# A two-stack transformer kernel: another entry to the first mixing layer, and the last output units by halves

## The chip, the cores and the metric

The kernel runs on one core of a Trainium2 chip. The metric is the device time of one execution in microseconds (us), as the median of several runs. The engines are called PE (TensorE's matmuls; PEld is its weight load), DVE (VectorE), ACT (ScalarE), POOL (GpSimd) and SP (SyncE, which only issues DMAs here). Each engine works through its own queue in order, and they meet at semaphores.

## The reference, cut to what matters

Two small transformers run one behind the other on 256 tokens of width 1024 (two token tiles of 128). The first has a pooling layer and an attention layer, each followed by a gated feed-forward (FFN) layer. The second has two "mixing" layers, again each with an FFN. The place that the change is about is where the two meet:

```python
# end of the first stack
x = x + swiglu(rmsnorm(x, norm_ffn[1]), ...)
x = rmsnorm(x, final_norm)
# start of the second stack
h = rms_norm(x, attn_norm[0])
proj = h @ w_in[0]
...
x = x + mix @ w_o[0]
```

Two norms stand here one behind the other. The kernel takes them together: with g the gain of `final_norm`, it needs mean(x²) and mean((x·g)²). The layer's input is x·g times a factor per token (from both sums) times the second gain; the residual stream is x·g times another factor per token (from mean(x²) alone).

## The kernel before

**Weights come in units.** All weights pass through three slots of 128x2048 floats (`raw`, loaded by SP's queue). ACT's `split` copies a unit rounded to `whi`, DVE subtracts (`wlo = raw - whi`, line 991), and PE multiplies the rounded and the rest part: three products in place of one. Slot of unit n is n % 3, so ACT may write `whi` of unit n only when PE has finished with unit n-3: `split` waits for the counter `units_used` (line 678 is its ACTIVATE). A load of unit n waits for DVE's subtraction of unit n-3. The latents' two units of a mixing layer are 1664 wide, all others 2048.

**End of a layer.** The last two units of every output product (of an FFN, lines about 1850, or of an attention, `last_two_by_tile`) are multiplied tile by tile. I call the first of the two units A and the last one B. For each tile and unit there are two halves of 512 columns with six matmuls each, so one tile is 24 matmuls. In tile 1 the order is A half 0, A half 1, B half 0, B half 1. `used` is counted for A when its half 1 is done. In five of the seven places the next layer's tile-0 transposes (line 1729) stand ahead of the last six matmuls. The two others are the end of FFN 1, ahead of the first mixing layer, where they come behind all of them, and the end of the kernel. DVE adds each finished half to `x` (`add_residual`, line 1001).

**Start of a layer.** ACT squares the halves of tile 0 (line 689, with a sum by row), then does the `split` of the new layer's second unit (which goes to the slot of A), then two copies of the transposed input, `h_out` (line 696, `h_both`), then tile 1's squares. DVE computes the mean square, POOL the power -0.5 (`rstd`), and DVE multiplies (`normalise`, line 1019) to `xn`, which PE transposes. PE's first pass over tile 0 needs both the rounded second unit (`hi_ready`) and tile 0's `h_out`.

**The first mixing layer's entry** (`final_norm_1` on DVE, the part `if l == 0` on ACT) is written by hand. DVE makes x·g into `xn` (line 1394), ACT squares halves of x and of x·g (line 866), DVE combines sums (lines 1400, 1403, 1404), POOL makes both factors at once (line 659), DVE multiplies `xn` in place (`mixer_input`, line 1412), and at the end four `residual_out` (line 1417) write the residual stream. PE's `latents` (line 1631) works through tile 0's three passes, with tile 1's transposes between them, then tile 1's.

SP's queue issues, behind unit 5 of this layer, two loads of score biases into `bias`, then unit 6.

Of the kernel before, what the change touches and what calls it, by code (L numbers as in the profile page):

```python
# [26 lines left out]
ALU = mybir.AluOpType  # L27
# [3 lines left out]
P = 128  # L31
T = 256
D = 1024
# [153 lines left out]
def bass_two_stacks(nc, a, c, out):  # L187
    ctx = ExitStack()
    with ctx:
# [27 lines left out]
        usq = sb("usq", [P, TT, 2])  # L217
# [52 lines left out]
        dsquare = xn[:, 0, HALF:D]  # L270
        bias_moba = bias[:, 0:16 * T].rearrange("p (h k) -> p h k", h=16)
# [169 lines left out]
        def _(sp):  # L441
# [110 lines left out]
            for l in range(2):  # L552
                for n in range(15):
# [116 lines left out]
        def _(act):  # L670
# [186 lines left out]
            def mix(l):  # L857
# [3 lines left out]
                if l == 0:  # L861
                    done = [16]

                    def next_square(src, t, h, acc):
                        act.wait_ge(squares, done[0])
                        act.activation(junk[:, :], src[:, t, h * HALF:(h + 1) * HALF], ACT.Square, scale=1.0 / 32,
                                       accum_out=acc[:, t, h:h + 1]).then_inc(squares, 1)
                        done[0] += 1

                    def square_x(t, h):  # L870
# [3 lines left out]
                        next_square(x, t, h, ssq)  # L874

                    def square_scaled(t, h):
                        act.wait_ge(scaled_ready, 2 * t + h + 1)
                        next_square(xn, t, h, usq)

                    for h in range(2):  # L880
                        square_x(0, h)
                        square_scaled(0, h)
                    split(u0 + 1)
                    h_out(6, 0, 0)
                    h_out(6, 0, 1)
                    square_x(1, 0)
                    square_x(1, 1)
                    square_scaled(1, 0)
                    square_scaled(1, 1)
                    for h in range(2):  # L890
                        h_out(6, 1, h)
# [3 lines left out]
                for ev in mix_script():  # L895
# [81 lines left out]
        def _(dve):  # L977
# [15 lines left out]
            def add_residual(version, t, h):  # L993

                if (t, h) == (1, 1):
                    dve.wait_ge(units_used, LAST_U[version] + 1)
                else:
                    dve.wait_ge(acc_ready, 3 * ACC_NO[version] + 2 * t + h + 1)
                xs = x[:, t, h * HALF:(h + 1) * HALF]
# [384 lines left out]
            def final_norm_1():  # L1384
# [3 lines left out]
                def scaled(t, h):  # L1388
                    cols = slice(h * HALF, (h + 1) * HALF)
                    if (t, h) == (0, 0):  # L1390
                        dve.wait_ge(gains_in[1], 16 * 3)
                        dve.wait_ge(xT_ready, 4 * (HT_NO[6] - 1))
                    dve.wait_ge(x_ready, 12 + 2 * t + h + 1)
                    dve.tensor_tensor(xn[:, t, cols], x[:, t, cols], gx[:, cols], ALU.mult).then_inc(scaled_ready, 1)

                def mean_squares(t):

                    dve.wait_ge(squares, 22 if t else 19)
# [4 lines left out]
                    then_wait(dve.tensor_scalar(msq[:, 6 + t:7 + t], msq[:, t:t + 1], EPS, usq[:, t, 0:1], ALU.mult, ALU.add))  # L1403
                    dve.tensor_tensor(msq[:, 6 + t:7 + t], msq[:, 6 + t:7 + t], usq[:, t, 1:2], ALU.add).then_inc(msq_ready, 1)

                def mixer_input(t, h):

                    cols = slice(h * HALF, (h + 1) * HALF)
                    if (t, h) == (0, 0):
                        dve.wait_ge(gains_in[0], 16 * 4)  # L1410
                    dve.wait_ge(rstd_ready, tile_no(5, t) + 1)
                    dve.scalar_tensor_tensor(out=xn[:, t, cols], in0=xn[:, t, cols], scalar=rstd[:, 6 + t:7 + t],
                                             in1=gz[:, cols], op0=ALU.mult, op1=ALU.mult).then_inc(xn_ready, 1)

                def residual_out(t, h):
                    cols = slice(h * HALF, (h + 1) * HALF)
                    dve.scalar_tensor_tensor(out=x[:, t, cols], in0=x[:, t, cols], scalar=rstd[:, t:t + 1],
                                             in1=gx[:, cols], op0=ALU.mult, op1=ALU.mult).then_inc(x_ready, 1)
# [744 lines left out]
```

## Time and profile before

| | us |
|---|---|
| median of 3 runs | 1132.6 |
| lowest, highest | 1132.23, 1134.55 |
| the profiled execution | 1133.23 |
| its span in the trace | 1131.4 |
| PE busy in it | 1116.1 (99%) |
| DVE busy | 783.3 (69%) |
| ACT busy | 533.9 (47%) |
| POOL busy | 109.0 (10%) |

The profiled execution took 1.8 us more than its span; that part lies outside the instructions. The mean granted TensorE clock was 0.997 of full speed. PE's stalls are few, so each engine's rows are read around those stalls and around places where another engine waits for PE.

### The profile page before, as it was taken

The page shows a single profiled execution, that of the slowest core. Times are in us where ns is not written, and L with a number is a line of the kernel's source. Part 1 is how long each engine was busy: PE and PEld are TensorE (multiplying, and loading weights), DVE is VectorE, ACT ScalarE, POOL GpSimd, SP SyncE. Part 2 cuts the span into 40 slices and gives each one's busy share as a digit, 9 for nine tenths or more (in the row PEclk, how much of TensorE's full clock was granted, in tenths as well). Part 3 has the DMA queues.
Part 4 walks back from the last instruction along what each step waited for, and adds up shares of the span by engine and source line. Part 5 has one row for each costly group of instructions (what it writes and reads, how often), then busy time and mean ns, then how long its engine had stood idle before and what let it go on. Part 6 is the DMA issues. An engine that isn't in the chain of part 4 may idle for free.

```text
span 1131.4 us, 16797 instructions
## 1 busy us (share of the span) xinstructions
PE 1116.1 (99%) x6452; PEld 970.6 (86%) x6452; DVE 783.3 (69%) x1022; ACT 533.9 (47%) x706; POOL 109.0 (10%) x200
## 2 busy tenths in 40 slices
PE   8999999999999999998999999999999999999997
PEld 7888888898888888887998888888899988888886
DVE  6766666767667666678677576666776866766665
ACT  5533333455654333345576543333456755333332
POOL 1000000000000000001770000000038400000000
PEclk9999999999999999999999999999999999999999
DMA  8765565663356555566963466565689444665551
GB/s 255 254 205 194 179 211 192 219 222 121 130 170 227 190 181 190 187 183 212 274 163 112 149 223 201 175 199 185 181 238 224 117 150 135 214 208 186 185 185 38
DMA packets 174152, 211.23 MB, mean 187 GB/s; under 512 B 22387, under 2 KB 157107, under 8 KB 174098
## 3 DMA queue, kind: packets, MB, share of 16 engines
q1 hardware_dynamic: 164322, 202.89, 56.9%
q0 software_dynamic: 9776, 7.62, 3.6%
q8 instruction: 35, 0.57, 0.2%
q14 instruction: 19, 0.16, 0.0%
HBM read 201.98 MB, written 1.16 MB: 180 GB/s over the span
## 4 chain that ended last, share of the span: by engine, by line
PE 94%; DVE 3%; ACT 1%; DMA 1%; issue 1%; POOL 0%; SPq 0%; DVEq 0%; POOLq 0%; ACTq 0%
PE bank L1592 25%; PE bank L1596 13%; PE bank L1566 13%; PE bank L1567 13%; PE bank L1568 13%; PE bank L1663 3%; PE bank L1872 2%; PE bank L1893 2%; PE bank L1605 1%; PE bank L1729 1%; PE bank L1903 1%; DMA raw<-in_pool_w 1%; DVE wlo L991 1%; PE bank L2112 1%; PE bank L1608 1%
## 5 line engine op out<-in xcount | busy, mean ns | idle before, releaser
L678 ACT ACTIVATE whi<-raw 128x2048 fp32r<-128x2048 f32 x178 | 338.8, 1907 | 383.1 <-PE bank L1596 245.5
L991 DVE TENSOR_TENSOR wlo<-raw,whi 128x2048 fp32r<-128x2048 f32 x172 | 393.0, 2287 | 151.0 <-ACT whi L678 151.0
L1592 PE MATMUL bank<-h_both,whi 128*128 128x512 f32 x1280 | 304.6, 390 | 0.0
L1592 PEld LDWEIGHTS bank<-h_both,whi 128*128 128x128 f32 x1280 | 237.7, 188 | 47.7
L1566 PE MATMUL bank<-whi,o_hi 128*128 128x512 f32 x448 | 176.2, 393 | 0.0
L1567 PE MATMUL bank<-wlo,o_hi 128*128 128x512 f32 x448 | 174.9, 390 | 0.0
L1568 PE MATMUL bank<-whi,o_lo 128*128 128x512 f32 x448 | 174.4, 389 | 0.0
L1596 PEld LDWEIGHTS bank<-h_both,wlo 128*128 128x128 f32 x1280 | 164.1, 191 | 6.2
L1596 PE MATMUL bank<-h_both,wlo 128*128 128x256 f32 x1280 | 166.0, 283 | 0.0
L1568 PEld LDWEIGHTS bank<-whi,o_lo 128*128 128x128 f32 x448 | 84.1, 188 | 18.0
L1566 PEld LDWEIGHTS bank<-whi,o_hi 128*128 128x128 f32 x448 | 84.3, 188 | 17.6 <-issue 1.3
L1567 PEld LDWEIGHTS bank<-wlo,o_hi 128*128 128x128 f32 x448 | 84.3, 188 | 15.5
L1190 DVE TENSOR_REDUCE pr<-bank 128x512 f32<-128x1024 f32 x40 | 49.0, 1224 | 47.6 <-PE bank L1596 47.6
L603 POOL TENSOR_TENSOR rstd<-msq,neghalf 128x1 f32<-128x1 f32 x16 | 9.2, 576 | 749.8 <-DVE msq L1007 749.8
L1195 DVE TENSOR_REDUCE pr<-bank 128x512 f32<-128x1024 f32 x36 | 44.1, 1225 | 43.1 <-PE bank L1596 43.1
L1566 PE MATMUL bank<-h_both,whi 128*128 128x256 f32 x192 | 55.3, 288 | 0.8 <-DVE wlo L991 0.8
L786 ACT ACTIVATE pr<-pr,negmax 128x256 f32<-128x256 f32 (+1 forms) x96 | 45.9, 480 | 19.3 <-DVE negmax L1277 19.3
L1567 PE MATMUL bank<-h_both,whi 128*128 128x256 f32 x192 | 54.3, 283 | 0.0
L1568 PE MATMUL bank<-h_both,wlo 128*128 128x256 f32 x192 | 54.3, 283 | 0.0
L1277 DVE CUSTOM_DVE_ANT_0 pr<-bank,bias 128x256 f32<-128x256 f32 (+1 forms) x96 | 32.8, 399 | 17.1 <-PE bank L1872 11.0
L1663 PE MATMUL bank<-whi,h_both 128*128 128x512 f32 x160 | 39.7, 395 | 0.4 <-ACT h_both L696 0.3
L1566 PE MATMUL bank<-whi,h_both 128*128 128x256 f32 (+1 forms) x128 | 38.9, 304 | 0.7 <-DVE h_both L1339 0.7
(201 smaller groups left out, 1335.3 us busy)
## 6 DMA issues: line engine op xcount, KB each, us to landing
raw<-in_w_gate_up SPq DMA_DIRECT2D x44, 1024.0 KB, 5.1
raw<-in_w_down SPq DMA_DIRECT2D x44, 1024.0 KB, 4.9
raw<-in_w_gate SPq DMA_DIRECT2D x22, 1024.0 KB, 5.4
raw<-in_w_up SPq DMA_DIRECT2D x22, 1024.0 KB, 5.4
raw<-in_w_in SPq DMA_DIRECT2D x18, 1024.0 KB, 7.4
raw<-in_w_o SPq DMA_DIRECT2D x12, 1024.0 KB, 5.5
raw<-in_w_kv SPq DMA_DIRECT2D x8, 1024.0 KB, 5.4
raw<-in_w_q SPq DMA_DIRECT2D x4, 1024.0 KB, 5.2
```

Of the source, the lines that this page charges most:

```text
L678: act.activation(whi[:, s, 0:w], raw[:, s, 0:w], ACT.Copy).then_inc(hi_ready, 1)
L786: e = act.activation(pr[:, s, q, 0:w], src, ACT.Exp, bias=negmax[:, s, q:q + 1], scale=-1.0 if biased else 1.0, accum_out=psumrow[:, s, q: ...
L991: dve.tensor_tensor(wlo[:, s, 0:w], raw[:, s, 0:w], whi[:, s, 0:w].bitcast(F32), ALU.subtract).then_inc(lo_ready, 1)
L1190: dve.tensor_reduce(gate32, halves(0), AX_X, ALU.add).then_inc(gate_sum, 1)
L1195: dve.tensor_reduce(up32, halves(2), AX_X, ALU.add).then_inc(up_sum, 1)
L1277: e = dve.tensor_tensor_reduce(pr[:, s, q, 0:w], bank[i % 2][:, q * T:q * T + w], biases[q], -1.0, BIG, ALU.add, ALU.min, negmax[:, s, q:q ...
L1566: pe.matmul(dst, ahi, bhi, start=first, stop=False)
L1567: pe.matmul(dst, ahi, blo, start=False, stop=False)
L1568: return pe.matmul(dst, alo, bhi, start=False, stop=last)
L1592: pe.matmul(bank[bk + jj][:, :], hi[:, kc, jj * P:(jj + 1) * P], h_both[:, kc, :, :].rearrange("p a t -> p (a t)"), start=(kc == 0), stop= ...
L1596: mm = pe.matmul(bank[bk + jj][:, T:2 * T], lo[:, kc, jj * P:(jj + 1) * P], h_hi[:, kc, :], start=False, stop=(kc == KC - 1))
L1663: mm = pe.matmul(bank[bk][:, :], h[:, kc, tile(t)], pair_of(w, n, kc), start=(first and kc == 0), stop=(last and kc == KC - 1))
```

## The change

It has two parts (the diff's pieces stand in the order buffer, SP, ACT, DVE, PE's latents, PE's last units of an attention; the end of an FFN gets the same order as these). **One**, at the first mixing layer's entry: x·g gets a buffer of its own, `x_gained`, in the first 2048 columns of `bias`; ACT squares a whole 1024-wide tile of it in one instruction (its output goes to `xn` as scratch), so one DVE combination falls away per tile; the four residual writes move from DVE to ACT, behind the latents' squares; DVE's and ACT's orders are rewritten; ACT's `split` of the second unit comes behind tile 1's sums; the latents' passes and transposes get another order; and SP's bias loads and the next `add_residual` wait for the residual writes. **Two**, at all ends of layers: tile 1's last two units go half by half, so the order is A half 0, B half 0, A half 1, (transposes), B half 1.

```diff
+        x_gained = bias[:, 0:TT * D].rearrange("p (t d) -> p t d", t=TT)
...
+                        sp.wait_ge(x_ready, 4 * 5)
                         for i, dst in ((0, bias_diff), (1, bias_dil)):
...
+                    def square_gained(t):
+                        if t == 0:
+                            act.wait_ge(xT_ready, 4 * (HT_NO[6] - 1))
+                        act.wait_ge(scaled_ready, 2 * t + 2)
+                        act.activation(xn[:, t, :], x_gained[:, t, :], ACT.Square, scale=1.0 / 32,
+                                       accum_out=usq[:, t:t + 1]).then_inc(squares, 2)
...
-                    for h in range(2):
-                        square_x(0, h)
-                        square_scaled(0, h)
-                    split(u0 + 1)
+                    square_x(0, 0)
+                    square_x(0, 1)
+                    square_gained(0)
+                    square_x(1, 0)
                     h_out(6, 0, 0)
                     h_out(6, 0, 1)
-                    square_x(1, 0)
                     square_x(1, 1)
-                    square_scaled(1, 0)
-                    square_scaled(1, 1)
-                    for h in range(2):
-                        h_out(6, 1, h)
+                    square_gained(1)
+                    split(u0 + 1)
+                    h_out(6, 1, 0)
+                    h_out(6, 1, 1)
...
+                        if l == 0:
+                            for t in range(TT):
+                                act.wait_ge(rstd_ready, tile_no(5, t) + 1)
+                                for h in range(2):
+                                    cols = slice(h * HALF, (h + 1) * HALF)
+                                    act.activation(x[:, t, cols], x_gained[:, t, cols], ACT.Copy, scale=rstd[:, t:t + 1]).then_inc(x_ready, 1)
...
                 split_half(MIX_U[0], 0)
                 mean_squares(0)
-                split_half(MIX_U[0], 1)
+                add_residual(4, 1, 0)
                 mixer_input(0, 0)
                 mixer_input(0, 1)
-                add_residual(4, 1, 0)
+                scaled(1, 0)
                 add_residual(4, 1, 1)
-                for h in range(2):
-                    h_lo_out(6, 0, h)
-                    scaled(1, h)
-                split_half(MIX_U[0] + 1, 0)
+                scaled(1, 1)
+                h_lo_out(6, 0, 0)
+                h_lo_out(6, 0, 1)
                 mean_squares(1)
-                split_half(MIX_U[0] + 1, 1)
-                for h in range(2):
-                    mixer_input(1, h)
-                for h in range(2):
-                    h_lo_out(6, 1, h)
-                for t in range(TT):
-                    for h in range(2):
-                        residual_out(t, h)
+                split_half(MIX_U[0], 1)
+                mixer_input(1, 0)
+                mixer_input(1, 1)
+                split(MIX_U[0] + 1)
+                h_lo_out(6, 1, 0)
+                h_lo_out(6, 1, 1)
...
+                if j == 6:
+                    wait_h(j, 0)
+                    latent_pass(u0, 0, h_lo, whi, range(KC))
+                    pe.wait_ge(lo_ready, u0 + 1)
+                    latent_pass(u0, 0, h_hi, wlo, range(0, LAT_K))
+                    transposes(j, 1)
...
-                for t in range(TT):
-                    for i in range(2):
-...
+                for i in range(2):
+                    pe.wait_ge(lo_ready, n + i + 1)
+                    pe.wait_ge(out_lo, ready[i])
+                    residual(n + i, chunks[i], O, False, i == 1, (0,))
+                for h in range(2):
+                    mm = residual(n, chunks[0], O, False, False, (1,), (h,))
+                    if h:
+                        used(mm)
+                        transposes(j, 0)
+                    mm = residual(n + 1, chunks[1], O, False, True, (1,), (h,))
+                used(mm)
```

ACT's queue at the first mixing layer's entry, before: the 1664-wide copy is the `split` of the layer's second unit.

```order
175 L866 ACTIVATE junk,ssq<-x 128x512 [waits squares,x_ready]
176 L866 ACTIVATE junk,usq<-xn 128x512 [waits squares,scaled_ready]
177 L678 ACTIVATE whi<-raw 128x1664 [waits units_used,raw_in0]
178 L696 ACTIVATE h_both<-bank 128x4x128 [waits xT_ready] x2
179 L866 ACTIVATE junk,ssq<-x 128x512 [waits squares,x_ready] x2
180 L866 ACTIVATE junk,usq<-xn 128x512 [waits squares,scaled_ready] x2
181 L696 ACTIVATE h_both<-bank 128x4x128 [waits xT_ready] x2
```

The same place after the change:

```order
175 L879 ACTIVATE xn,usq<-bias 128x1024 [waits scaled_ready,xT_ready]
176 L871 ACTIVATE junk,ssq<-x 128x512 [waits squares,x_ready]
177 L698 ACTIVATE h_both<-bank 128x4x128 [waits xT_ready] x2
178 L871 ACTIVATE junk,ssq<-x 128x512 [waits squares,x_ready]
179 L879 ACTIVATE xn,usq<-bias 128x1024 [waits scaled_ready]
180 L680 ACTIVATE whi<-raw 128x1664 [waits units_used,raw_in0]
181 L698 ACTIVATE h_both<-bank 128x4x128 [waits xT_ready] x2
```

The copy of the second unit stood ahead of tile 0's `h_out` and now stands behind them and behind tile 1's sums.

PE's queue from the first latents' pass on, before (`h_both` with `whi` or `wlo` are the latents' passes, `ident,xn` the transposes of tile 1):

```order
923 L1631 MATMUL bank<-whi,h_both 128x416 [waits hT_hi,hi_ready]
924 L1631 MATMUL bank<-whi,h_both 128x416 x3
925 L1631 MATMUL bank<-whi,h_both 128x416 [waits hT_hi]
926 L1631 MATMUL bank<-whi,h_both 128x416 x3
927 L1631 MATMUL bank<-wlo,h_both 128x416 [waits lo_ready]
928 L1631 MATMUL bank<-wlo,h_both 128x416 x3
929 L1631 MATMUL bank<-whi,h_both 128x416 [waits hT_lo]
930 L1631 MATMUL bank<-whi,h_both 128x416 x3
931 L1729 MATMUL bank<-ident,xn 128x128 [waits xn_ready]
```

And after:

```order
923 L1632 MATMUL bank<-whi,h_both 128x416 [waits hT_hi,hi_ready]
924 L1632 MATMUL bank<-whi,h_both 128x416 x3
925 L1632 MATMUL bank<-whi,h_both 128x416 [waits hT_hi]
926 L1632 MATMUL bank<-whi,h_both 128x416 x3
927 L1632 MATMUL bank<-whi,h_both 128x416 [waits hT_lo]
928 L1632 MATMUL bank<-whi,h_both 128x416 x7
929 L1632 MATMUL bank<-wlo,h_both 128x416 [waits lo_ready]
930 L1632 MATMUL bank<-wlo,h_both 128x416 x3
931 L1738 MATMUL bank<-ident,xn 128x128 [waits xn_ready]
```

Four more matmuls now stand ahead of tile 1's transposes; the first row waits for the same two semaphores as before, of which `hi_ready` is given by the copy that moved on ACT.

PE's queue at the end of FFN 0, tile 1, before (rows 230 to 235 are A half 0, row 242 begins B half 0):

```order
240 L1567 MATMUL bank<-wlo,o_hi 128x512
241 L1568 MATMUL bank<-whi,o_lo 128x512
242 L1566 MATMUL bank<-whi,o_hi 128x512 [waits act_ready]
243 L1567 MATMUL bank<-wlo,o_hi 128x512
244 L1568 MATMUL bank<-whi,o_lo 128x512
```

After, B half 0 begins at row 236 and A half 1 at row 242:

```order
234 L1568 MATMUL bank<-wlo,o_hi 128x512
235 L1569 MATMUL bank<-whi,o_lo 128x512
236 L1567 MATMUL bank<-whi,o_hi 128x512 [waits act_ready]
237 L1568 MATMUL bank<-wlo,o_hi 128x512
238 L1569 MATMUL bank<-whi,o_lo 128x512
```

B's first half moved six matmuls forward and A's second half six back. The transposes stay at row 248 in both, and so A is finished at row 247 in place of row 241.

## Rows read from the trace of the kernel before

**Rows 1.** The page: its first line, the span.

```profile
span 1131.4 us, 16797 instructions
```

**Rows 2.** PE's waits, whole span: line, waited for; us, times, longest.

```profile
PE bank L1729 <- DVE xn L1412: 3.7, 2, 3.4
...
PE bank L1566 <- DVE wlo L991: 0.8, 1, 0.8
```

**Rows 3.** PE's timeline, end of FFN 1: start, us, line [idle before <-releaser].

```profile
506.60 0.39 PE L1568 MATMUL bank<-whi,o_lo 128*128 128x512 f32 x1
...
507.96 0.39 PE L1568 MATMUL bank<-whi,o_lo 128*128 128x512 f32 x1
```

**Rows 4.** ACT's timeline at the attention layer's entry (end of FFN 0).

```profile
208.02 1.92 ACT L678 ACTIVATE whi<-raw 128x2048 fp32r<-128x2048 f32 x1 [1.33 <-PE bank L1568]
209.85 1.06 ACT L696 ACTIVATE h_both<-bank 128x512 fp32r<-128x512 f32 x2
```

**Rows 5.** PE's timeline at the same entry.

```profile
209.13 1.03 PE L1729 MATMUL bank<-ident,xn 128*128 128x128 f32 x8
211.38 3.79 PE L1663 MATMUL bank<-whi,h_both 128*128 128x512 f32 x16
...
215.58 0.66 PE L1729 MATMUL bank<-ident,xn 128*128 128x128 f32 x4
```

**Rows 6.** DVE's timeline at the same entry.

```profile
210.97 1.28 DVE L1026 TENSOR_TENSOR h_both<-bank,h_both 128x512 fp32r<-128x512 f32 x2
...
214.77 1.41 DVE L1019 SCALAR_TENSOR_TENSOR xn<-x,rstd,gains 128x512 f32<-128x512 f32 x2 [0.66 <-POOL rstd L603]
```

**Rows 7.** ACT's timeline at the second mixing layer's entry.

```profile
817.52 1.60 ACT L678 ACTIVATE whi<-raw 128x1664 fp32r<-128x1664 f32 x1 [1.33 <-PE bank L1568]
```

**Rows 8.** DVE's timeline at the end of the kernel.

```profile
1125.19 0.69 DVE L1001 TENSOR_TENSOR x<-x,bank 128x512 f32<-128x512 f32 x1 [0.67 <-PE bank L1568]
```

**Rows 9.** PE's timeline at the first mixing layer's entry.

```profile
508.71 1.32 PE L1729 MATMUL bank<-ident,xn 128*128 128x128 f32 x8 [0.36 <-DVE xn L1412]
510.14 1.74 PE L1631 MATMUL bank<-whi,h_both 128*128 128x416 f32 x8
...
516.75 1.02 PE L1729 MATMUL bank<-ident,xn 128*128 128x128 f32 x4 [3.36 <-DVE xn L1412]
...
523.81 1.66 PE L1631 MATMUL bank<-wlo,h_both 128*128 128x416 f32 x8
526.27 0.39 PE L1566 MATMUL bank<-h_both,whi 128*128 128x256 f32 x1 [0.80 <-DVE wlo L991]
...
532.93 0.36 PE L1566 MATMUL bank<-h_both,whi 128*128 128x256 f32 x1
```

**Rows 10.** Stretches there: PE, PEld, DVE, ACT, POOL busy (instructions), PEclk, DMA, GB/s.

```profile
513.40:516.70 3.30, 0.00 (x0) 0.00 (x0) 2.64 (x7) 0.32 (x2) 1.35 (x1) 1.00 0.09 11
...
517.40:518.90 1.50, 1.50 (x6) 1.38 (x5) 0.47 (x1) 0.60 (x1) 0.00 (x0) 0.50 1.01 358
```

**Rows 11.** ACT's timeline at the first mixing layer's entry.

```profile
505.06 0.63 ACT L866 ACTIVATE junk<-xn 128x512 bf16<-128x512 f32 x1
...
517.80 0.60 ACT L696 ACTIVATE h_both<-bank 128x512 fp32r<-128x512 f32 x1 [4.09 <-PE bank L1729]
...
526.28 3.71 ACT L678 ACTIVATE whi<-raw 128x2048 fp32r<-128x2048 f32 x2
```

**Rows 12.** DVE's timeline at the first mixing layer's entry.

```profile
505.89 0.21 DVE L1403 TENSOR_SCALAR msq<-msq,usq 128x1 f32<-128x1 f32 x1 [0.40 <-ACT junk L866]
...
506.21 1.02 DVE L1036 TENSOR_TENSOR wlo<-raw,whi 128x832 fp32r<-128x832 f32 x1
507.90 1.41 DVE L1412 SCALAR_TENSOR_TENSOR xn<-xn,rstd,gains 128x512 f32<-128x512 f32 x2 [0.67 <-POOL rstd L659]
...
521.28 2.73 DVE L1417 SCALAR_TENSOR_TENSOR x<-x,rstd,gains 128x512 f32<-128x512 f32 x4
```

**Rows 13.** POOL's timeline at the first mixing layer's entry.

```profile
506.45 1.35 POOL L659 TENSOR_TENSOR rstd<-msq,neghalf 128x2 f32<-128x2 f32 x1 [179.30 <-DVE msq L1404]
...
527.23 1.01 POOL L638 TENSOR_TENSOR rstd<-msq,neghalf 128x4 f32<-128x4 f32 x1 [11.32 <-DVE msq L1468]
```

**Rows 14.** SP's queue at the same place.

```profile
531.89 2.57 SPq L449 DMA_DIRECT2D raw<-in_w_in  x2
```

More of the change, by code:

```diff
@@ L1637, in latents @@
                 latent_pass(u0, 0, h_hi, whi, range(KC), first=True, j=j)
-                pe.wait_ge(lo_ready, u0 + 1)
-                latent_pass(u0, 0, h_hi, wlo, range(0, LAT_K))
-                wait_h(j, 0)
-                latent_pass(u0, 0, h_lo, whi, range(0, 4))
-                transposes(j, 1, (0,))
-                latent_pass(u0, 0, h_lo, whi, range(4, KC))
-                transposes(j, 1, (1,))
+                if j == 6:
[4 more added lines that the diff above has]
+                    transposes(j, 1)
+                else:
+                    pe.wait_ge(lo_ready, u0 + 1)
+                    latent_pass(u0, 0, h_hi, wlo, range(0, LAT_K))
+                    wait_h(j, 0)
+                    latent_pass(u0, 0, h_lo, whi, range(0, 4))
+                    transposes(j, 1, (0,))
+                    latent_pass(u0, 0, h_lo, whi, range(4, KC))
+                    transposes(j, 1, (1,))
                 latent_pass(u0, 1, h_hi, whi, range(KC), first=True, j=j)
@@ L1686, in last_two_by_tile @@
             def last_two_by_tile(n, chunks, ready, j):
-                for t in range(TT):
-                    for i in range(2):
-                        if t == 0:
-                            pe.wait_ge(lo_ready, n + i + 1)
-                            pe.wait_ge(out_lo, ready[i])
-                        mm = residual(n + i, chunks[i], O, False, i == 1, (t,), j if t and i else None)
-                        if t:
-                            used(mm)
+                for i in range(2):
[9 more added lines that the diff above has]
+                used(mm)
             def token_major(n, bk, col, width, t, src, wcols):
@@ L1702, in token_major, with residual @@
                 return mm
-            def residual(n, chunks, src, first, last, tiles=range(TT), before_last=None):
+            def residual(n, chunks, src, first, last, tiles=range(TT), hs=range(2)):
                 hi, lo = w2(n)
                 for t in tiles:
-                    for h in range(2):
-                        if before_last is not None and h:
-                            transposes(before_last, 0)
+                    for h in hs:
                         for k in range(2):
@@ L1846, in ffn @@
                 gate_up(b, 2)
-                for t in range(TT):
-                    if t == 0:
-                        pe.wait_ge(act_ready, e0 + b)
-                    pe.wait_ge(lo_ready, u0 + 2 + 3 * b + t)
-                    mm = residual(u0 + 1 + 3 * b, 2, O, False, False, (t,))
-                    if t:
+                before, after = u0 + 1 + 3 * b, u0 + 2 + 3 * b
+                pe.wait_ge(act_ready, e0 + b)
+                pe.wait_ge(lo_ready, before + 1)
+                residual(before, 2, O, False, False, (0,))
+                pe.wait_ge(act_tile0, f + 1)
+                pe.wait_ge(lo_ready, after + 1)
+                residual(after, 0, O, False, True, (0,))
+                for h in range(2):
+                    mm = residual(before, 2, O, False, False, (1,), (h,))
+                    if h:
                         used(mm)
-                    if t == 0:
-                        pe.wait_ge(act_tile0, f + 1)
-                        pe.wait_ge(lo_ready, u0 + 3 + 3 * b)
+                        if f in (0, 2):
+                            transposes({0: 2, 2: 8}[f], 0)
                     else:
                         pe.wait_ge(act_ready, e0 + b + 1)
-                    mm = residual(u0 + 2 + 3 * b, 0, O, False, True, (t,), {0: 2, 2: 8}.get(f) if t else None)
+                    mm = residual(after, 0, O, False, True, (1,), (h,))
                 used(mm)
```

33 lines of the change are left out of this document (13 added, 20 removed).

## The prediction

> **What bounds the kernel now.** I read the page first: the span is 1131.4 us [rows 1], and PE is busy for 99% of it by the table above. So only two things move the time: PE's own idle time, and its clock. I then read PE's waits. The reader is to see how little there is to win: the two places that the change aims at cost 3.7 and 0.8 us [rows 2], both at the first mixing layer's entry. PE's timeline there shows them: 0.36 us ahead of tile 0's transposes, 3.36 us ahead of tile 1's, 0.80 us ahead of unit 2 [rows 9]. Then the granted clock: it is 1.00 in the idle stretch and 0.50, which is the 1.2 GHz level, in 517.4 to 518.9, just behind the 3.36 us without a matmul [rows 10]. Last I looked for engines that wait for PE, since the change reorders PE's work at the end of every layer. ACT's copy of the second unit idles 1.33 us for a PE matmul at the attention layer's entry [rows 4] and does so in all five places where the transposes stand between the last matmuls (the second mixing layer's is [rows 7], the other three are FFN entries). That row decides this prediction.
>
> **Part two, the last units by halves: a loss at five entries.** Matmuls of 512 columns are 0.227 us apart: six take from 506.60 to 507.96, 1.36 us [rows 3]. B half 0 is finished 1.36 us earlier. What does that give? DVE's add of that half stands behind the normalised tile 0 in its queue, or, at the FFN entries, starts up to 0.35 us earlier and is then followed by work that waits for ACT; no PE wait ends on it. At the kernel's end the last add is released by the very last matmul [rows 8], whose place is the same. Gain 0. A's half 1 is finished 1.36 us later. ACT's copy into A's slot starts at 208.02 now, released by A, and is 1.92 long; `h_out` starts at 209.85 directly behind it, though the transposes it reads began at 209.13 [rows 4, 5]. So the copy just fits ahead of `h_out`. Moved by 1.36 it starts at 209.38 and ends at 211.30; `h_out` half 0 runs 211.21 to 211.81 (0.60 by [rows 11]); PE's first pass starts some 0.14 us behind such a copy's end, at 211.95. It starts at 211.38 now [rows 5]. PE stalls 0.57 us. Both engines that wait are in order, and nothing on PE's queue can go ahead: behind the first pass stands the whole layer.
>
> The tile-1 chain at that entry adds to it: DVE's h_lo rows start at 210.97 now [rows 6]; they wait for `h_out` and so start at 211.84, 0.87 us later, and behind them stand the add of tile 1's half 1, a half split, the mean square, POOL, and the `xn` row at 214.77. Its first half is ready at 215.52 and PE takes it at 215.58 [rows 5, 6], with no slack: so this entry is delayed by 0.87 to 0.9 us in all, not 0.57. At the three FFN entries tile 1's `xn` has slack, so 0.57 each. At the second mixing layer the copy is 1.60 long [rows 7], so the first pass loses only 0.57 - 0.32 = 0.25, but tile 1's chain is delayed by 0.5 and has no slack there: 0.5. Sum: 0.9 + 3 x 0.57 + 0.5 = 3.1 us, each a real PE stall, none absorbed later because PE waits nowhere else.
>
> **Part one, the mixing layer's entry.** Worked through queue by queue. Tile 0: a 512-wide square is 0.63 [rows 11], and a copy of 1664 takes 0.32 less than one of 2048 [rows 4, 7], so 512 elements more cost 0.43 and a 1024-wide square 1.06. ACT squares the two halves of x, then x·g from 504.56 to 505.6; its sum comes 0.1 earlier than now, one small DVE step (0.25 with its gap) falls away, and `xn` starts at 507.6 in place of 507.90 [rows 12]. The transposes start at 508.4 (508.71 now). The 0.36 us idle shrinks to about 0.1.
>
> Then the moved copy: ACT does h_out twice (to 510.3), the square of x half (1,1) from 510.26, x·g of tile 1 from 511.08 to 512.14, and only then the 1.60 us copy, 512.18 to 513.78. PE's first latents' pass waits for it, at 513.9; it started at 510.14 [rows 9]. So the 3.36 us wait for tile 1's `xn` is not removed but exchanged for one of about 4.0 us (509.9 to 513.9), one step earlier in the queue. What is won is that tile 1's `xn` is ready at 514.9 and 515.6, so nothing waits later: 20 matmuls of 0.19 to 0.20 us [rows 9] to 517.8, transposes to 518.7, a 0.4 us wait for `h_out`, 28 more matmuls to 524.5. The second unit's rest part and unit 2's are ready (517.4 and 523.8), since the residual's 2.73 us [rows 12] left DVE. Unit 2 starts at 524.5 in place of 526.27 [rows 9]: 1.8 earlier, if the clock is full.
>
> The residual is now on ACT: four copies of 0.6, 2.1 us with overlap, between the latents' squares and the copies of units 3 and 4. These began at 526.28, 1.0 us behind the latents' end [rows 11]. Now unit 3's begins 3.1 us behind it, at 527.5, ends at 529.4, DVE's subtraction at 531.7 (2.3 long). PE is there at 524.5 + (532.93 - 526.27) = 531.1 [rows 9]: a new stall of about 0.6 us. Unit 3 starts at 531.77 in place of 532.93, so the entry gives 1.2 us at full clock. SP's new wait holds the two bias loads and unit 6's load behind them until about 527.7; they take 2.6 us to issue, and unit 6's load goes at 531.89 today [rows 14], so it isn't late: 0.
>
> The clock: 3.36 us of idle was followed by 0.50, which cost half of some 3.4 us, 1.7 us at most [rows 10]. A 4.0 us idle should be followed by the same, now right on the passes of tile 0, where no slack remains. Bounds 0 and 1.7; I take 1.5, since the new gap is longer than the one that did it. The entry is then 0.3 us slower than before; at the bounds 1.2 faster or 0.5 slower.
>
> One rule speaks on POOL's step. Row 506.45 is 1.35 us for two columns while DVE subtracts two SBUF operands beside it (506.21, 1.02 us); row 527.23 is 1.01 us for four columns with DVE idle [rows 12, 13]. By that, tile 0's step without such a neighbour could take 0.7 to 1.0 in place of 1.35, and the change puts an add from PSUM beside it. ACT's chain, and the first pass, would come about 0.35 us earlier. The Trainium skill (SBUF — State Buffer, Who interferes with whom) says that a VectorE instruction with two SBUF inputs contends with a GpSimd instruction that reads SBUF; by it the sum would be 0.35 less.
>
> **The sum.** 3.1 - 1.2 + 1.5 = 3.4 us on the profiled execution of 1133.23 (span 1131.4): 1136.6. That execution lay 0.6 above the median of 1132.6, so for a median I take 1136.0.
>
> **Rivals.**
> The clock stays full. For it: its drop followed a single idle stretch in this trace, and the runs before spread from 1132.2 to 1134.6. Against it: the new gap is longer. It gives 1132.6 + 3.1 - 1.2 = 1134.5. This is the case that ends on the other side, not slower by what can be measured; it decides at whether the 4.0 us without a matmul brings the 0.50.
> The five entries are covered: if ACT's copy and h_out went faster or PE's pass waited for something else anyway. For it: `h_out` half 0 need be only 0.57 earlier. Against it: rows 4 and 5 fit to 0.1 us. It gives 1132.6 + 0.3 = 1132.9, and with a full clock 1131.4.
> POOL's step shortens at tile 0: evens, but it moves only 0.35, to 1135.6, and stays within each case.
> ACT becomes the bound: if the residual copies delay units 3 to 5 by another 1 to 2 us, at the point from which unit 4's copy too comes late. It gives 1137.5 to 1138. Against it: each later unit has the matmuls of the one ahead of it as cover, 5.9 us and more.
>
> **How the numbers follow.** My forecast (entries lose, clock drops, 1136.0) 0.58; full clock 0.18; entries covered 0.12; ACT the bound 0.08; both good cases together or something that I miss 0.04. A measurement can tell about 0.2%, 2.3 us, from no change: the border is 1134.9. Slower: nearly all of the forecast and of the ACT case, and a third of the full-clock case, 0.70. Within: 0.27. Faster: 0.03. The range leaves out the covered entries and the far end: 1133.8 to 1137.6.
>
> **What would show it.** Right: ACT's 2048-wide copy at the five entries idles 2.7 us for PE in place of 1.33, and PE's rows show 0.5 to 0.9 us idle ahead of each first pass or of tile 1's transposes; PE's 3.36 us wait is gone, and a wait of about 4 us for ACT's `whi` stands ahead of the first latents' pass; the clock is 0.50 right behind it; a wait of 0.6 us for `wlo` ahead of unit 3. Wrong: no idle at the five entries (then the first term fails), or an idle under 3 us at the latents (then ACT's order was misread), or a granted clock of 1.00 throughout.

## The result, and the profile after

The changed kernel takes 1136.81 us (median of ten runs, 1135.98 to 1137.92) against 1132.54 for the one before (ten runs beside them). The ratio is 1.0038, with a 95% interval of 1.003 to 1.0046: 4.3 us slower. The profiled execution took 1137.92, at the upper end of its own spread, with a span of 1136.1; its difference from the profiled one of before is 4.7 us. One of the eight executions of after_held below took 1226.29 us at a granted clock of 0.85; its ratio leaves it out, and without it its median would be 1134.92 in place of 1134.96.

The page after. The busy row of each engine:

```profile
PE 1118.8 (98%) x6452; PEld 972.3 (86%) x6452; DVE 780.4 (69%) x1015; ACT 534.8 (47%) x706; POOL 108.5 (10%) x200
```

PE is busy 2.7 us longer than before with the same matmuls to do, so part of the 4.7 us is slower matmuls and only the rest is waiting. PE's waits, whole span (line and what it waited for: us, times, longest), to be held against [rows 2]:

```profile
PE bank L1632 <- ACT whi L680: 3.9, 1, 3.9
PE bank L1671 <- ACT h_both L698: 1.9, 5, 0.4
...
PE bank L1738 <- DVE xn L1029: 1.0, 2, 0.6
PE bank L1567 <- DVE wlo L999: 0.9, 1, 0.9
```

The 3.36 us wait for tile 1's `xn` is gone. In its place stands one of 3.9 us for the moved copy, and four of the five waits for `h_both` are new (the fifth, 0.34 us, is near the start of the kernel in both).

**The five entries.** ACT's timeline at the attention layer's entry, to be held against [rows 4] (start, us, engine, line, operation [idle before <-releaser]):

```profile
209.29 1.92 ACT L680 ACTIVATE whi<-raw 128x2048 fp32r<-128x2048 f32 x1 [2.70 <-PE bank L1569]
211.12 1.06 ACT L698 ACTIVATE h_both<-bank 128x512 fp32r<-128x512 f32 x2
```

And PE's timeline there, against [rows 5]:

```profile
209.03 1.03 PE L1738 MATMUL bank<-ident,xn 128*128 128x128 f32 x8
...
211.84 3.92 PE L1671 MATMUL bank<-whi,h_both 128*128 128x512 f32 x16 [0.39 <-ACT h_both L698]
...
216.33 0.66 PE L1738 MATMUL bank<-ident,xn 128*128 128x128 f32 x4
...
325.94 3.95 PE L1671 MATMUL bank<-whi,h_both 128*128 128x512 f32 x16 [0.39 <-ACT h_both L698]
```

The last row is the same pass at the entry to FFN 1. The copy idles 2.70 us in place of 1.33. The execution enters this place 0.10 us earlier than the one before did (209.03 for 209.13) and tile 1's transposes come 0.75 later, so the entry costs 0.85. Read in the same way, the entry to FFN 1 begins 0.77 late, its tile-1 transposes are 1.47 late (328.73 became 330.20), and so it costs 0.70. The entry to FFN 2 costs 0.70, the second mixing layer's 0.52 (there PE idles 0.40 ahead of tile 1's transposes, for 0.19 before) and that to FFN 3 0.72. Together 3.5 us.

**The first mixing layer's entry.** PE's timeline, after, against [rows 9]:

```profile
509.67 1.04 PE L1738 MATMUL bank<-ident,xn 128*128 128x128 f32 x8
514.57 5.91 PE L1632 MATMUL bank<-whi,h_both 128*128 128x416 f32 x16 [3.86 <-ACT whi L680]
520.28 1.17 PE L1632 MATMUL bank<-wlo,h_both 128*128 128x416 f32 x4
521.29 1.03 PE L1738 MATMUL bank<-ident,xn 128*128 128x128 f32 x8
...
535.65 0.39 PE L1567 MATMUL bank<-h_both,whi 128*128 128x256 f32 x1 [0.91 <-DVE wlo L999]
```

Stretches there (PE, PEld, DVE, ACT, POOL busy with instructions, PEclk, DMA, GB/s), against [rows 10]:

```profile
513.50:514.00 0.50, 0.00 (x0) 0.00 (x0) 0.50 (x1) 0.50 (x1) 0.50 (x1) 0.97 0.00 0
514.00:515.00 1.00, 0.43 (x1) 0.43 (x2) 0.41 (x2) 0.52 (x1) 0.85 (x1) 0.50 0.00 0
...
519.00:520.50 1.50, 1.50 (x6) 1.43 (x5) 0.00 (x0) 0.00 (x0) 0.00 (x0) 0.50 0.94 148
520.50:521.00 0.50, 0.50 (x3) 0.48 (x3) 0.00 (x0) 0.00 (x0) 0.00 (x0) 0.71 0.78 138
```

The clock was full until the very end of the idle stretch and then 0.50 from 514.0 to about 520.8, 6.8 us, nearly all of it over matmuls. Unit 3 starts 2.72 us later than before, and it entered with 1.47, so this place costs 1.25.

### The profile page after: what moved, and what is told of

It reads as the page before. It is cut to its first block, busy times and chain, and to the rows that moved or that the text cites. A ratio compares the mean times of both kernels' runs of the same rounds, so it can differ in the third digit from the quotient of the medians.

```text
span 1136.1 us, 16789 instructions
## 1 busy us (share of the span) xinstructions
PE 1118.8 (98%) x6452; PEld 972.3 (86%) x6452; DVE 780.4 (69%) x1015; ACT 534.8 (47%) x706; POOL 108.5 (10%) x200
## 4 chain that ended last, share of the span: by engine, by line
PE 93%; DVE 2%; ACT 2%; issue 1%; DMA 1%; POOL 0%; SPq 0%; DVEq 0%; POOLq 0%; ACTq 0%
PE bank L1593 25%; PE bank L1597 13%; PE bank L1567 13%; PE bank L1568 13%; PE bank L1569 13%; PE bank L1671 3%; PE bank L1884 2%; PE bank L1905 2%; PE bank L1632 2%; PE bank L1606 1%; PE bank L1915 1%; ACT whi L680 1%; DVE wlo L999 1%; DMA raw<-in_pool_w 1%; PE bank L1738 1%
## 5 line engine op out<-in xcount | busy, mean ns | idle before, releaser
L999 DVE TENSOR_TENSOR wlo<-raw,whi 128x2048 fp32r<-128x2048 f32 (+1 forms) x173 | 395.0, 2285 | 152.0 <-ACT whi L680 151.9
L1567 PEld LDWEIGHTS bank<-whi,o_hi 128*128 128x128 f32 x448 | 84.3, 188 | 17.5 <-issue 1.3
```

The costliest lines, as they stand in the source:

```text
L999: dve.tensor_tensor(wlo[:, s, 0:w], raw[:, s, 0:w], whi[:, s, 0:w].bitcast(F32), ALU.subtract).then_inc(lo_ready, 1)
L1567: pe.matmul(dst, ahi, bhi, start=first, stop=False)
```

## Experiments

Each is told with the edit, what was expected of it, what it measured beside runs of the kernel before on the same chip, and what follows. The medians of before in these comparisons lie between 1132.59 and 1132.63.

**The two parts apart: part1_only and part2_only.** The first is the changed kernel with the end of every layer as before, the second the kernel before with the new ends. The edit of the first at one of the two functions, the FFN's end being treated alike:

```diff
-                for h in range(2):
-                    mm = residual(n, chunks[0], O, False, False, (1,), (h,))
-                    if h:
-                        used(mm)
-                        transposes(j, 0)
-                    mm = residual(n + 1, chunks[1], O, False, True, (1,), (h,))
+                for t in range(TT):
+                    for i in range(2):
...
```

> The new entry of the first mixing layer alone; the last output units are multiplied in the order of before. Theory (the 3.5 us of the trace outside this entry come from the last units' new order, which holds ScalarE's copy of the next layer's second unit back): the loss shrinks to what the entry costs, +0.5 to +1.5 us against before, and ScalarE's copies at the other five entries idle 1.33 us again. Rival (the new order of the last units is neutral, the entry and its clock drop cost everything): +4 us, as after the whole change.

> The last output units by halves alone; the mixing layer's entry as before. Theory: five entries at 0.5 to 0.9 us each, +3.1 to +3.5 us against before; ahead of the first mixing layer, where no transposes stand between the matmuls, nothing or up to 0.2 us either way. Rival (neutral order): within 0.5 us of before, or faster, since TensorE gives half a tile 1.36 us earlier.

Measured: part1_only 1133.79, ratio 1.0017 (1.0008 to 1.0026), 1.2 us more by medians. part2_only 1136.4, ratio 1.0033 (1.0021 to 1.0046), 3.8 us more, for 3.1 to 3.5 expected. PE's timeline of part1_only (eleven of the pass's sixteen matmuls fall into this view), and its clock:

```profile
513.50 3.78 PE L1632 MATMUL bank<-whi,h_both 128*128 128x416 f32 x11 [3.99 <-ACT whi L680]
...
518.81 1.03 PE L1737 MATMUL bank<-ident,xn 128*128 128x128 f32 x8
```

```profile
513.50:516.50 3.00, 3.00 (x9) 2.87 (x10) 2.68 (x3) 0.00 (x0) 0.29 (x1) 0.50 0.64 186
```

Part two is most of the loss. Part one alone exchanges the wait, as expected, and the clock falls behind it, here for 3.4 us. In part2_only the copy at the attention entry idles 2.70 us and PE waits 1.9 us for `h_both` in five places, the same rows as in the changed kernel. The two parts alone add up to 5.0 us, and the whole change costs 4.3: together they share a gain, worked out below under B's half 0.

**Part two at chosen places: part2_ffn13 and part2_ffn0.** The kernel before, with the new order only at the ends of FFN 1 and 3 (`f in (1, 3)`), where no transposes stand between the last matmuls, and only at the end of FFN 0 (`f == 0`).

```diff
+                if f in (1, 3):
...
+                    for h in range(2):
+                        mm = residual(before, 2, O, False, False, (1,), None, (h,))
...
+                        mm = residual(after, 0, O, False, True, (1,), None, (h,))
+                    used(mm)
+                else:
```

> The last output units by halves only at the end of FFN 1 and FFN 3, where no transposes stand between the last matmuls and ScalarE's copy of the next second unit isn't what the first pass waits for. Theory: 0 +- 0.3 us against before. Rival (the halves' order is itself slower, or itself faster, wherever it stands): 2 of 7 places, so about 2/7 of what part 2 alone gives, +1 us or more.

> The last output units by halves at the end of FFN 0 only. Theory: this entry alone costs 0.85 us (0.39 us ahead of the first pass, the rest ahead of tile 1's transposes), 1133.3 to 1133.6 us. Rival: 0 here and all of it elsewhere.

Measured: part2_ffn13 1132.41, ratio 0.9999 (0.999 to 1.0007). part2_ffn0 1133.3, ratio 1.0012 (1.0002 to 1.0021), 0.7 us more. ACT and PE of part2_ffn0 at the attention entry:

```profile
208.49 1.92 ACT L678 ACTIVATE whi<-raw 128x2048 fp32r<-128x2048 f32 x1 [2.70 <-PE bank L1568]
```

```profile
211.03 3.91 PE L1663 MATMUL bank<-whi,h_both 128*128 128x512 f32 x16 [0.39 <-ACT h_both L696]
...
215.53 0.66 PE L1729 MATMUL bank<-ident,xn 128*128 128x128 f32 x4
```

One changed end gives one entry its loss. Here the transposes of tile 0 start at 208.23 and those of tile 1 7.30 us later; before, it was 6.45 [rows 5], so 0.85. The other four ends, unchanged, show none. The new order is not bad by itself: where no copy stands ahead of `h_out` in a tight chain, it costs nothing.

part2_ffn13 showed something else. Its PE waits the same 3.36 us as before for tile 1's `xn`, but the stretch behind it reads:

```profile
516.03 0.66 PE L1729 MATMUL bank<-ident,xn 128*128 128x128 f32 x4 [3.36 <-DVE xn L1412]
```

```profile
516.00:517.50 1.50, 1.47 (x10) 1.42 (x11) 0.78 (x2) 0.60 (x1) 0.00 (x0) 1.00 0.80 238
```

The clock stayed at 1.00, where before it was 0.50 behind an equally long wait [rows 10]. From those transposes to unit 2 this execution took 8.12 us (516.03 to 524.15), the one before 9.52 [rows 9]: the half clock had cost it 1.40. The executions without a profile fit this. 58 other executions of the kernel before, taken beside these experiments, lie between 1130.73 and 1134.86 us: the 21 with a mean granted clock of 0.998 have a median of 1131.74 us, the 14 with 0.996 one of 1133.09, 1.35 more. So the clock doesn't fall in every execution of the same kernel.

**A larger dose of the late release: part2_a_last.** part2_only with A's half 1 last of all, behind the transposes, so that ACT's copy is released by the layer's last matmul.

```diff
+                residual(n, chunks[0], O, False, False, (1,), (0,))
+                residual(n + 1, chunks[1], O, False, True, (1,), (0,))
+                residual(n + 1, chunks[1], O, False, False, (1,), (1,))
+                transposes(j, 0)
+                residual(n, chunks[0], O, False, True, (1,), (1,)).then_inc(units_used, 2)
```

> The last output units by halves alone, with A's half 1 at the very end, behind B's half 1: it is finished another six matmuls, 1.36 us, later. Same matmuls, same place of the transposes. Theory (each entry's stall is the delay of ScalarE's copy less what cover there is): 5 x 1.36 = 6.8 us on top of part 2 alone, about 1143 us, and that copy idles 4.0 to 4.1 us at the five entries in place of 2.70. Rival (the stalls come from the order of accumulating into the banks, not from the copy): within 1 us of part 2 alone.

Measured: 1150.14, ratio 1.0159 (1.0145 to 1.0173), 17.5 us more than before and well beyond what I expected. ACT at the attention entry, and PE's first pass there (213.88) and at the entry to FFN 2 (644.85):

```profile
211.34 1.91 ACT L678 ACTIVATE whi<-raw 128x2048 fp32r<-128x2048 f32 x1 [4.95 <-PE bank L1568]
```

```profile
213.88 3.88 PE L1663 MATMUL bank<-whi,h_both 128*128 128x512 f32 x16 [2.64 <-ACT h_both L696]
...
644.85 5.50 PE L1663 MATMUL bank<-whi,h_both 128*128 128x512 f32 x16 [2.64 <-ACT h_both L696]
```

The mechanism held: five waits for `h_both`, now 2.3 to 2.6 us each. Two sizes were wrong. First, A's half 1 moved behind the eight transposes too, which take 0.79 us of PE (209.03 to 209.82 in the changed kernel), so the copy starts 2.23 us later than in part2_only (211.34 for 209.11), not 1.36. Five times 2.23 on 1136.4 is 1147.6. Second, behind two of the five waits the clock fell: the sixteen matmuls at 644.85 take 5.50 us where those at 213.88 take 3.88, and the eight of the second mixing layer's first pass 2.82 where the changed kernel needs 1.75. That adds 2.7 us, 1150.2 in all, and closes the sum. So with the release late enough the loss follows it one for one, and the half clock can follow an idle stretch of 2.3 to 2.6 us too.

**The clock, with PE kept working: after_held and before_held.** The changed kernel with fourteen matmuls of 512 columns between tile 0's transposes and the first latents' pass, and the kernel before with twelve ahead of tile 1's transposes. They write to a bank that holds nothing then and their results are used by nothing; no other work is left out or moved.

```diff
+                if j == 6:
+                    for _i in range(14):
+                        pe.matmul(bank[3][:, :], o_lo[:, 0, 0:P], o_lo[:, 0:2, :], start=True, stop=True)
```

> The changed kernel with 14 matmuls of 512 columns (3.2 us, results unused, into a bank that the next transposes overwrite) in the idle stretch ahead of the first latents' pass. They fit into the 3.9 us, so they take no time of their own. Theory (the clock falls to 1.2 GHz in that stretch and stays there for up to 6.9 us, at a cost of up to 3.1 us): 1.5 to 3.1 us faster than the changed kernel, about 1134 to 1135 us, and a granted clock of 1.00 behind the stretch. Rival (the clock is incidental; the chain through ScalarE and VectorE sets the time): within 0.5 us of the changed kernel.

> The kernel of before with 12 matmuls of 512 columns (2.7 us, results unused) in its 3.36 us wait ahead of tile 1's transposes. Theory (the clock's drop there costs up to 1.4 us, but not in every execution: a run of nearly the same code showed 1.00 behind the same wait): a median 0.3 to 1.4 us below before, 1131.2 to 1132.3 us, clock 1.00 behind the stretch. Rival (no cost, since VectorE's chain ends later anyway): within 0.2 us of before.

Measured: after_held 1134.96, ratio to before 1.0023 (1.0012 to 1.0034), 1.85 us less than the changed kernel's 1136.81. before_held 1131.42, ratio 0.9992 (0.9983 to 1.0001), 1.2 us less by medians with an interval that just takes in no change. PE in after_held:

```profile
510.38 3.43 PE L1639 MATMUL bank<-o_lo 128*128 128x512 f32 x14
514.49 3.28 PE L1632 MATMUL bank<-whi,h_both 128*128 128x416 f32 x16 [0.68 <-ACT whi L680]
517.60 0.91 PE L1632 MATMUL bank<-wlo,h_both 128*128 128x416 f32 x4
518.35 0.82 PE L1741 MATMUL bank<-ident,xn 128*128 128x128 f32 x6
```

```profile
514.40:518.40 4.00, 3.91 (x21) 3.84 (x22) 3.22 (x3) 0.04 (x1) 0.36 (x1) 1.00 0.78 232
```

The first pass starts at the same time as in the changed kernel (514.49 and 514.57), since it waits for the same copy, but the sixteen matmuls take 3.28 us for 5.91, with the clock at 1.00. From there to tile 1's transposes it is 3.86 us here and 6.72 in the changed kernel's profile: the half clock cost that execution 2.86 us. In part1_only, with half clock for 3.4 us, the same way took 5.31, so 1.45. Useless work in the gap is worth 1.85 us by medians. It need not help in every execution: five took 1134.47 to 1134.99 us with a mean granted clock of 0.998 or 0.999, and two took 1136.33 and 1136.43 with 0.997.

**ACT's order: part1_early.** part1_only with ACT's copy of the second unit directly behind the square of x·g of tile 0, where it finds the slot's unit long used, in place of behind tile 1's sums.

```diff
                     square_gained(0)
+                    split(u0 + 1)
...
                     square_gained(1)
-                    split(u0 + 1)
```

> The new entry alone (last output units as before), with ScalarE's copy of the second unit back ahead of tile 0's copies, behind the first tile's sums. Theory (that copy's place makes the 4.0 us wait, and the wait makes the clock drop): TensorE's first latents' pass starts some 4 us earlier, the only long wait left is about 1.1 us ahead of tile 1's transposes, the clock stays at 1.00, unit 3 still waits 0.7 to 0.9 us for its rest part; about 4 us faster than part 1 alone and 3 to 3.7 us faster than before, 1129 to 1129.6 us. Rival (tile 1's sums set the entry whatever the copy's place): the wait moves back ahead of the transposes at 3 us or more and the time stays within 1 us of part 1 alone.

Measured: 1129.26, ratio 0.9969 (0.9958 to 0.998): 4.5 us less than part1_only, 3.4 less than before. ACT and PE:

```profile
505.41 1.59 ACT L680 ACTIVATE whi<-raw 128x1664 fp32r<-128x1664 f32 x1
...
508.81 1.26 ACT L698 ACTIVATE h_both<-bank 128x512 fp32r<-128x512 f32 x2 [0.65 <-PE bank L1737]
```

```profile
509.55 1.74 PE L1632 MATMUL bank<-whi,h_both 128*128 128x416 f32 x8
511.90 1.77 PE L1632 MATMUL bank<-whi,h_both 128*128 128x416 f32 x8 [0.62 <-DVE h_both L1036]
513.51 0.92 PE L1632 MATMUL bank<-wlo,h_both 128*128 128x416 f32 x4
514.55 1.32 PE L1737 MATMUL bank<-ident,xn 128*128 128x128 f32 x8
...
529.04 0.38 PE L1567 MATMUL bank<-h_both,whi 128*128 128x256 f32 x1 [0.91 <-DVE wlo L999]
```

The copy ends at 507.00, and ACT still idles 0.65 ahead of `h_out`: the move costs nothing there. Up to unit 3, whose 0.91 us wait for `wlo` is still there (529.04), PE has no wait over 0.62 us, and the mean granted clock is 0.999, for 0.997 before. This is what part one was worth without its late copy; of the 3.4 us some 1.2 (before_held) to 1.4 (part2_ffn13) are the half clock that the kernel before had at this place, so the order itself gives about 2. The wait that I expected ahead of tile 1's transposes did not come; one of 0.62 for DVE's `h_lo` stands ahead of them instead, and with it the ready time is covered.

**The residual's place: early_late_copies.** part1_early with ACT's four residual copies moved behind the copy of unit 3.

```diff
+                        if l == 0 and ev[1] == 3:
+                            for t in range(TT):
...
-                        if l == 0:
-                            for t in range(TT):
...
```

> The same, and ScalarE's four residual copies moved behind its copy of unit 3. Theory (these copies are what holds unit 3's rest part back): the 0.9 us wait ahead of unit 3 goes, 0.6 to 0.9 us faster than part1_early. Rival (VectorE's latent rows are late anyway): no more than 0.2 us.

Measured: 1128.16, ratio 0.9964 (0.995 to 0.9978), 1.1 us less than part1_early (0.6 to 0.9 expected). Unit 3, which waited 0.91 for `wlo` in the changed kernel and in part1_early, goes straight on:

```profile
527.83 0.38 PE L2051 MATMUL bank<-ident,xn 128*96 128x128 f32 x2
527.97 0.36 PE L1567 MATMUL bank<-h_both,whi 128*128 128x256 f32 x1
```

From FFN 1's last matmul to unit 3 it is 20.25 us in this profile (507.72 to 527.97) and 21.40 in part1_early's (507.64 to 529.04). So the residual copies ahead of units 3 and 4 were a bad price for the time taken off DVE; a little later nobody waits for them.

**Halves at one end only: early_late_best.** early_late_copies with the new order at the end of FFN 1 alone, which part2_ffn13 had shown to cost nothing, the condition being `f == 1`.

> The same again, and the last output units by halves at the end of FFN 1 only, ahead of this entry. Half a tile comes 1.36 us earlier, where VectorE's new order adds it while GpSimd computes. Theory: 0.1 to 0.4 us faster than early_late_copies. Rival (as everywhere else, this order only holds ScalarE's copy back): that copy now starts up to 1.2 us later but still ends ahead of tile 0's transposes, so 0.

Measured: 1128.35, ratio 0.9964 (0.995 to 0.9978), no gain over early_late_copies by medians, of five executions each. ACT shows why tile 0 gains nothing:

```profile
506.40 1.60 ACT L680 ACTIVATE whi<-raw 128x1664 fp32r<-128x1664 f32 x1 [1.43 <-PE bank L1569]
```

The early copy is released by A, and A is finished later, so `h_out` and the first pass come no earlier, though `xn` does (PE waits 0.69 us there). This is the mechanism of part two again, and at tile 0 it takes back what the earlier half gives. Tile 1's chain keeps a part: from FFN 1's last matmul to unit 3 it is 19.94 us (507.28 to 527.22) for 20.25 in early_late_copies. These 0.3 us lie in the 0.1 to 0.4 expected, and the medians are too few to show them.

**POOL without its neighbour: pool_alone.** early_late_copies with DVE's subtraction of the first unit's second half ahead of tile 1's mean square, and one `h_lo` (an operand from PSUM, one from SBUF) beside POOL's step; PE takes the passes of tile 0 in the order in which these come.

```diff
                 scaled(1, 1)
+                split_half(MIX_U[0], 1)
                 h_lo_out(6, 0, 0)
-                h_lo_out(6, 0, 1)
                 mean_squares(1)
-                split_half(MIX_U[0], 1)
+                h_lo_out(6, 0, 1)
```

> The kernel early_late_copies with VectorE's half subtraction moved from beside GpSimd's tile-1 step to ahead of it, with TensorE's passes of tile 0 in an order to match. Theory (that step takes 1.35 us only because VectorE reads two operands from SBUF beside it; alone or beside a PSUM operand it takes 0.70, as tile 0's did): 0.70 to 0.75 us for tile 1's step too, and 0.2 to 0.5 us faster than early_late_copies. Rival (1.35 is the step's own length in tile 1): no change.

Measured: 1127.68, ratio 0.9962 (0.995 to 0.9975), 0.5 us less than early_late_copies by medians, though the five executions of each overlap (1127.51 to 1128.79, and 1128.06 to 1129.79). POOL's tile-1 step, first in early_late_copies, then in pool_alone:

```profile
512.44 1.35 POOL L661 TENSOR_TENSOR rstd<-msq,neghalf 128x2 f32<-128x2 f32 x1 [5.84 <-DVE msq L1412]
```

```profile
512.33 0.70 POOL L661 TENSOR_TENSOR rstd<-msq,neghalf 128x2 f32<-128x2 f32 x1 [6.18 <-DVE msq L1412]
```

The same instruction takes 0.70 in place of 1.35 when the subtraction is not beside it, and from FFN 1's last matmul to unit 3 it is 19.93 us (507.27 to 527.20), 0.3 less than in early_late_copies. This version has the lowest median: 4.9 us under the kernel before and 9.1 under the changed one.

## Why the prediction was right, point by point

**The forecast** was 1136.0 in 1133.8 to 1137.6, slower. It is 1136.81 and slower, and the rows that I named are there but for one size: I named 0.5 to 0.9 us idle ahead of the first passes or of tile 1's transposes, and the profile shows 0.39 and 0.40. Counted from start to start it is 0.54, as the next paragraph says. The three terms, against the profiled executions: 3.1 - 1.2 + 1.5 = 3.4 was forecast, and 3.5 - 1.6 + 2.9 = 4.8 is what the rows give for the 4.7 measured. So each term was too small; the first two errors, 0.4 each, cancel by luck, and what is left of the difference is the clock's. For the profiled execution itself my sum gave 1136.6, and it took 1137.92.

**The entries (3.1, measured 3.5).** The step from 1.33 to 2.70 of ACT's idle came to 0.01 us as worked out, and the entry where tile 1's chain has no slack costs 0.85, for 0.87 to 0.9. part2_ffn0 gives the same 0.85 from one changed end, part2_ffn13 gives none where the prediction says none, and part2_a_last shows a larger delay passed on in full. Mis-sized were the FFN entries, 0.57 each, where 0.70 was measured: the first pass comes 0.54 later as forecast, but its sixteen matmuls then take 3.95 us for 3.79. The trace shows where: at the entry to FFN 1 the second of them starts 0.31 us behind the first and the ninth 0.27 behind the eighth, where without the stall all follow at 0.22 to 0.23; behind the 2.64 us idle of part2_a_last the second starts 0.30 behind the first. So about half of it comes with the first matmul behind a stall. The rest I did not test.

**"Gain 0" for B's half 0 (wrong at one end).** At the end of FFN 1, on top of part one, the earlier half is worth 0.66. In part1_only DVE waits 1.05 us for that half with its add and the normalised tile 0 stands behind it, at 507.39; set against the layer's end this is 0.66 later than in the changed kernel. Tile 0's transposes gain only 0.23 of it, as they stand behind PE's last matmul; but tile 1's adds, its sums and so the moved copy stand behind `xn` on DVE and ACT, and the first latents' pass comes 0.64 earlier. I had only looked at DVE's order before the change. It was there to be seen in the order after, where the add stands ahead of `mixer_input(0, 0)`.

**The entry at full clock (-1.2, measured -1.6).** Part one's own share is right: in part1_only unit 3 starts 0.23 later than before [rows 9] on a layer that came 0.24 earlier (207.78 for 208.02 [rows 4]), 0.47 in all, and less the clock's 1.45 that is -1.0. The residual copies took 2.55 us, not 2.1, so the stall ahead of unit 3 was 0.91 for 0.6. The rest of the -1.6 is the 0.66 above. The reader should know what this term is set against: rows of before that hold 1.40 us of half clock themselves. With the full clock on both sides the changed entry gains only 0.2 us, and the change adds 1.5 of half clock (2.86 for 1.40), not 2.9. The loads on SP's queue cost nothing, as forecast.

**POOL (a rival, and it acted).** Its tile-0 step in the changed kernel is 0.71 us, with DVE's add from PSUM beside it, and the tile-1 step, with the subtraction of two SBUF operands beside it, is 1.35. pool_alone turned the second into 0.70 by giving it another neighbour. In part1_only tile 0's step is 0.71 with nothing on DVE beside it. The Trainium skill (SBUF — State Buffer, Who interferes with whom) says that a VectorE instruction with two SBUF inputs contends with a GpSimd instruction that reads SBUF; these rows agree. The price of such an overlap here is 0.65 us. I had given it 0.35 and left it out of the sum. What the shorter step at tile 0 is worth in the changed kernel's time no run separates.

**The clock (1.5, measured 2.9 in the profiled execution).** That it would fall was right, and 1.5 fits part1_only (1.45) and the kernel before (1.40). The step that failed is the bound: "0 and 1.7", taken from one stretch of 3.4 us. In the changed kernel's profile the half clock lasted twice as long. By medians the gap's clock costs 1.85 (after_held), so the profiled execution was on the dear side; that goes the way of the 4.7 there against 4.3 in the medians, but no run shows that it is the reason. Why it lasts 3.4 us in one execution and 6.8 in another stays open. What the rows show to differ is when it began: in the changed kernel 0.6 us ahead of the first matmul behind the gap (513.97 and 514.57), in part1_only 0.25 ahead, and in the kernel before 0.14 behind it.

**The other rivals.** The full clock is what after_held shows when PE is kept working: 1134.96, for 1134.5 worked out. Entries covered and ACT the bound did not happen.

## What to carry to other kernels

When the order of an engine's last matmuls is changed, ask not which result comes earlier but which buffer comes free later, and what stands behind the copy that waits for it on its in-order engine: 1.36 us on a release cost 0.5 to 0.85 us at each of five entries. A wait that is moved to another place is not removed; the copy that caused it had a place on the same engine, further ahead, where it cost nothing and the kernel was 4.5 us faster. And where PE is 99% busy, its longest single idle can be dearer than it looks: behind it the half clock cost 1.4 us more in one profiled execution and 2.9 in another.

## What the runs showed of the hardware

- The half clock behind one idle stretch lasted 3.4 us (part1_only, 3.99 us idle) and 6.8 us (the changed kernel, 3.86 us idle), in the second case while PE worked without a gap from 514.57 on.
- 3.36 us without a matmul were followed by the half clock in the kernel before and by none in part2_ffn13. Over 58 executions of the kernel before, those with the highest mean clock took 1.35 us less than those with 0.996. Of five stretches of 2.3 to 2.6 us in part2_a_last two were followed by it. So the length of the idle alone did not decide.
- Twelve or fourteen matmuls in the gap, with 0.62 and 0.68 us left idle, kept the clock at 1.00 in the two profiled executions. Two other executions of after_held had a mean of 0.997 and took some 1.5 us more.
- A two-column power on POOL is 0.70 us alone or beside a DVE operation with one operand in PSUM, and 1.35 us beside one with both in SBUF.
